# Distance-bias rows: one product for eight heads, and a store that repeats each row 128 times

## The reference

```python
bias_a = rel_bias[:, :A_HEADS]          # (32, 8)
bias_b = rel_bias[:, A_HEADS:]          # (32, 8)
...
bias = bias_table[t5_bucket(jnp.maximum(qpos[None, :, None] - sel, 0))]
s = jnp.where(valid[:, :, None, :], s + jnp.moveaxis(bias, -1, 2).astype(jnp.float32), NEG)
...
score = jnp.einsum('bqhs,bqh->bqs', jax.nn.relu(logits).astype(jnp.float32), wi)
_, sel = lax.top_k(score, topk)         # branch B: 256 keys for each query
```

## Time and profile before

| what | before |
|---|---|
| median of 3 timed runs | 3599.59 us (3599.34 to 3600.98) |
| profiled execution, its own time | 3594.39 us |
| its span, first to last instruction | 3592.7 us |
| mean granted TensorE clock | 0.968 of full |
| TensorE busy with matmuls | 3371.7 us, 94% |
| stores to `skew_scratch` | 4 of 768 KB, 3.4 us from issue to landing (median) |
| where the 16 bias products lie | 1953.5 to 1972.7 us of the span |

### The profile page before, as it was taken

How to read it: one execution, slowest core, us unless ns; L and a number is a source line. 1 busy time by engine, 2 the same in 40 slices (tenths; PEclk the granted TensorE clock), 3 DMA queues, 4 the chain that set the end, 5 groups by cost and what they waited for, 6 DMA issues and landing times.

```text
span 3592.7 us, 46841 instructions
## 1 busy us (share of the span) xinstructions
PE 3371.7 (94%) x19401; PEld 2566.3 (71%) x19401; DVE 1625.5 (45%) x3386; ACT 1121.9 (31%) x2273; POOL 457.7 (13%) x729
## 2 busy tenths in 40 slices
PE   8999999999998989999978999899999999999997
PEld 6775876777587657767646688678844588888886
DVE  3533444353344434534551699766721333323324
ACT  4432442243244333313333223366600211111112
POOL 0210120021012243203241122000000000000000
PEclk9999999999999989999987999999999999999999
DMA  2210110110011001101112123200040011111111
GB/s 97 72 36 12 42 43 1 36 28 33 18 36 42 19 15 42 42 18 42 54 39 75 37 88 94 94 1 1 1 188 12 30 48 47 59 47 48 47 47 47
DMA packets 40079, 159.61 MB, mean 44 GB/s; under 512 B 5335, under 2 KB 10009, under 8 KB 34362
## 3 DMA queue, kind: packets, MB, share of 16 engines
q1 hardware_dynamic: 39866, 156.62, 13.0%
HBM read 136.68 MB, written 19.92 MB: 44 GB/s over the span
## 4 chain that ended last, share of the span: by engine, by line
PE 78%; DVE 12%; ACT 4%; POOL 2%; issue 2%; DMA 1%; SPq 0%; POOLq 0%; ACTq 0%; DVEq 0%
PE pp L547 8%; PE pp L549 8%; PE pp L548 8%; PE pp L1180 7%; PE pp L1182 7%; PE pp L1181 7%; PE pp L717 5%; DVE xT L2224 4%; PE pp L1162 3%; PE pp L1152 3%; PE pp L868 3%; PE pp L1119 2%; PE pp L1103 2%; DVE arena L2224 2%; PE pp L647 1%
## 5 line engine op out<-in xcount | busy, mean ns | idle before, releaser
L547 PE MATMUL pp<-gx_hi,pw_hi 128*128 128x512 f32 x1616 | 664.4, 411 | 38.6 <-DVE pw_lo L1779 28.4
L549 PE MATMUL pp<-gx_hi,pw_lo 128*128 128x512 f32 x1616 | 641.2, 397 | 0.0
L548 PE MATMUL pp<-gx_lo,pw_hi 128*128 128x512 f32 x1616 | 640.4, 396 | 0.0
L547 PEld LDWEIGHTS pp<-gx_hi,pw_hi 128*128 128x128 f32 x1616 | 310.4, 192 | 113.5 <-DVE pw_lo L1779 31.6
L549 PEld LDWEIGHTS pp<-gx_hi,pw_lo 128*128 128x128 f32 x1616 | 309.4, 191 | 68.0
L548 PEld LDWEIGHTS pp<-gx_lo,pw_hi 128*128 128x128 f32 x1616 | 310.8, 192 | 60.3
L1180 PE MATMUL pp<-x_hi,wt_hi 128*128 128x512 f32 x704 | 274.1, 389 | 1.1 <-DVE x_lo L2353 1.1
L1182 PE MATMUL pp<-x_hi,wt_lo 128*128 128x512 f32 x704 | 273.9, 389 | 0.0
L1181 PE MATMUL pp<-x_lo,wt_hi 128*128 128x512 f32 x704 | 273.9, 389 | 0.0
L717 PE MATMUL pp<-xT,arena 128*128 128x512 f32 x512 | 233.8, 593 | 6.3 <-DVE arena L1955 6.3
L1779 DVE TENSOR_TENSOR pw_lo<-arena,pw_hi 128x1024 fp32r<-128x1024 f32 x73 | 89.6, 1229 | 237.9 <-ACT pw_hi L1235 237.9
(11 more groups left out here) (422 smaller groups left out, 6015.1 us busy)
## 6 DMA issues: line engine op xcount, KB each, us to landing
arena<-in_tiles_dram SPq DMA_DIRECT2D x73, 512.0 KB, 3.6
arena<-in_units_dram SPq DMA_DIRECT2D x33, 1024.0 KB, 4.9
xT<-in_tiles_dram SPq DMA_DIRECT2D x27, 512.0 KB, 4.2
xT<-in_w_outs_dram SPq DMA_DIRECT2D x6, 2048.0 KB, 8.1
arena<-gates_scratch SPq DMA_DIRECT2D x16, 512.0 KB, 4.6
gates_scratch<-arena SPq DMA_DIRECT2D x11, 512.0 KB, 5.2
arena<-in_xT_dram SPq DMA_DIRECT2D x8, 512.0 KB, 7.8
y<-in_x_dram SPq DMA_DIRECT2D x1, 4096.0 KB, 14.2
```

Source lines behind the costliest of these rows:

```text
L547: mm(b[:, hs], wh[:, c], X[0][:, k, hs], k == 0, False)
L548: mm(b[:, hs], wh[:, c], X[1][:, k, hs], False, False)
L549: m = mm(b[:, hs], wl[:, c], X[0][:, k, hs], False, k == 7)
```

## The change

The two edits belong together. A product now takes eight columns of `relb` as its stationary operand and gives eight different rows, one per partition, in 8 partitions; so there are two products (one per branch) in place of sixteen. The 128-fold repetition, which the product did before over the partitions, is now done by the store: its source is 8 partitions x 384, with a step of zero 128 times in between, and its destination the same 8 x 128 x 384 elements in DRAM as before. There are two such stores of 1536 KB in place of four of 768 KB.

```diff
-        vec = [aqT.rearrange("p t c -> p (t c)")[:, i * 1536:(i + 1) * 1536].rearrange("p (h c) -> p h c", h=4) for i in range(2)]
+        vec = [aqT[0:8, i, 0:384] for i in range(2)]
...
-            ring = Ring([4, 5])
-            for hd in range(16):
-                b = place_(ring, ("rb", hd), ("vec", hd))
-                pe.wait_ge(("d", "relb"), ("d", "oh0"), ("d", "oh1"))
-                mm(b[:, 0:384], relb[0:33, hd:hd + 1].to_broadcast([33, 128]), onehot[hd // 8], True, True).then_inc(*did("rb", hd))
+            for a in range(2):
+                b = place_(Ring([4 + a]), ("rb", a), ("vec", a))
+                pe.wait_ge(("d", "relb"), ("d", f"oh{a}"))
+                mm(b[0:8, 0:384], relb[0:33, 8 * a:8 * a + 8], onehot[a], True, True).then_inc(*did("rb", a))
...
-            for hd in range(16):
-                ac.wait_ge(("rb", hd), ("skew", hd // 4 - 2) if hd >= 8 else None)
-                act(vec[hd // 4 % 2][:, hd % 4, :], at("rb", hd)[:, 0:384], ACT.Copy).then_inc(*did("vec", hd))
+            for a in range(2):
+                evict(vec[a], at("rb", a)[0:8, 0:384], ("vec", a), ("rb", a))
...
-                    evict(aqT[:, u - 79, :], b, name, ("proj", u, 1), ("skew", 2), ("skew", 3))
+                    evict(aqT[:, u - 79, :], b, name, ("proj", u, 1), ("skew", 0), ("skew", 1))
...
-            for q in range(4):
-                sp.wait_ge(("vec", 4 * q + 3))
-                move(skew[4 * q:4 * q + 4].rearrange("h p c -> p h c"), vec[q % 2], f"skew{q % 2}", "skew", q)
+            for a in range(2):
+                sp.wait_ge(("vec", a))
+                move(skew[8 * a:8 * a + 8], vec[a].unsqueeze(1).to_broadcast([8, 128, 384]), f"skew{a}", "skew", a)
...
-                    sp.wait_ge(("skew", 2), ("skew", 3), [("ys", n) for n in range(8)])
+                    sp.wait_ge(("skew", 1), [("ys", n) for n in range(8)])
...
-            sp.wait_ge(("proj", 100, 1))
+            sp.wait_ge(("proj", 100, 1), ("skew", 0))
```

## The result

The changed kernel is slower: a median of 3607.95 us over 10 runs (3602.12 to 3612.47) against 3599.47 us over 10 runs for the kernel before, timed beside it. Two of those ten, of 4931.57 and 6839.76 us, lie far out and are not in the ratio. The ratio is 1.0024, with a 95% interval from 1.0015 to 1.0032, so +8.6 us with +5.4 to +11.5.

A forecast was written before the change was run, and what follows sets the result against it. It took TensorE, busy 94% of the span, as the bound, with tile 80's load setting the time after the change. 7.5 - 1.2 + 1.7 = +8.0 us on 3599.6 gave 3607.6, say 3608; range 3578 to 3615 us.

The forecast's parts named there:

- What TensorE saves: Bias products at L972: two in place of sixteen save 19.6 us on TensorE, with 17.9 and 21.3 as ends.
- full gain: Rival: stores read at 203 GB/s or faster, tile 80 is in time, the whole saving stands; 3580 us, chance 0.20.
- The rate of the stores: Two bias-row stores out of partitions 0 to 7: 50.8 GB/s, so 61.9 us for both.
- Tile 80 behind the stores: Tile 80's load queues behind the stores and lands at 2019.5; ACT's split of it runs 7.5 us later than before.
- One sign: On SP: both stores issued by 1956, and tile 80's load at 1959, 19.6 us earlier than before.
- Slack and restart: Index scores after tile 80's split: buffer slack used up, -1.2 us; TensorE restarting slowly after its idle time, +1.7 us.
- The rest moves with it: After the index scores: bisection begins at about 2049 in place of 2041; stretches from 2045 to 2275 keep their length.
- The other wait: Rival: tile 80 overtakes the stores, and copying out tile 79 into aqT waits for them instead; 3587 us, chance 0.05.
- A single share: Rival: the eight source partitions give 25.4 GB/s in all, tile 80 lands 69.5 us late; 3670 us, chance 0.10.

The follow-up runs named there:

- the dose between: Changed kernel with branch B's store reading every second of partitions 0 to 15, branch A's store unchanged; ratio 0.9973 against the kernel before.
- the other room: Changed kernel with the bias rows in the mask room of SBUF, so copying out tiles 79 to 82 waits for no store; ratio 1.0019 against the kernel before.
- step of 8: Changed kernel with each branch's eight rows in partitions 0, 8 to 56; 3579.39 us in one profiled execution, against a median of 3601.93 before.

## Why the prediction was right

The prediction said 3608 us with the chance of 0.45 for slower, and 3607.95 was measured. That they meet within a tenth of a us is luck, since the interval of the measurement is 6 us wide and the terms of the sum were off by up to 0.9 us each; that the path is the one that was foretold is not. Its steps:

- **What TensorE saves.** Ends of 17.9 and 21.3 us, 19.6 taken. Measured 17.8 at the split of tile 79: the lower end. The clock fell behind the two products too. Two stretches of the changed kernel, with the columns of the earlier trace rows:

```profile
1962.00:1968.00 6.00, 5.45 (x18) 3.10 (x16) 1.00 (x2) 2.35 (x5) 2.37 (x1) 0.50 0.41 48
1968.00:1970.00 2.00, 2.00 (x10) 1.24 (x7) 0.68 (x2) 0.61 (x1) 0.00 (x0) 0.88 0.43 50
```

  It stood at 0.50 until about 1968.5, some 7 us, as long as behind the sixteen products. The product price of 0.65 us held (1.38 us for two). The 1.8 us by which the term was too large did not matter, since the load and not TensorE set the time; it would have in a kernel with the full gain.
- **The rate of the stores.** 50.8 GB/s was chosen and 51.4 measured (3.146 MB over 61.2 us). That the number met is luck in part: the prediction had bounds of 25 and 203 GB/s from its rows and took two shares of eight partitions by judgement, while the share that counts is that of four neighbours. This term decided between 3580 and 3670 us. The four kernels with other source partitions, and branch B's store in the dose between, show the mechanism: the groups of partitions, not the engines, not the repetition, not the rows. The Trainium skill's 27.2 GB/s for each port (SBUF — State Buffer, Door 1, the DMA port swizzle) gave an estimate of 57.8 us and 3603.5 us; the measurement lies at 25.7 for each, and decides.
- **Tile 80 behind the stores.** Expected to land 64.6 us after the first store's issue, so that the split runs 7.5 us later than before; measured 64.5 us and 7.4. Two small errors cancel in it: data began 1.4 us after the issue, not 0.9, and streamed 61.2 us, not 61.9. That it is the queue is shown by the stores in ACT's queue. One sign did not come: both stores were to be issued by 1956 and tile 80 at 1959; on the old time line SP was busy with the pair until 1964.5, and with tile 80's issue until 1994.9. It changed nothing in the sum, because the end of the stores sets the landing.
- **Slack and restart.** -1.2 was expected for the slack and -1.4 measured (from +7.4 at the split to +6.0 at the scores). For the restart +1.7 was expected and +2.6 measured (from +6.0 to +8.6 where the bisection begins); the clock was 0.63 over the 6.6 us behind the restart, a loss of 2.4:

```profile
2028.40:2035.00 6.60, 6.60 (x18) 3.52 (x19) 4.00 (x6) 1.59 (x2) 0.93 (x2) 0.63 0.29 88
```

- **The rest moves with it.** +8.6 where the bisection begins, +7.2 at its end, +8.6 in the timed ratio. The bisection itself took 245.1 us here, 246.5 before and 248.1 with the rows in 128 partitions. Why it differs by some microseconds was not tried.
- **Rivals.** The full gain is what four kernels with other partitions show, and fails here by the rate alone. The other wait (copying out of tile 79) is excluded by the other room. A single share is excluded by the plateau.

What stays open: the kernel with 128 partitions gained 22.3 us by the ratio, and the end of its interval, 17.6, only just takes in the 17.8 that its trace shows at the split of tile 80. Its profiled span is 18.8 us shorter, but the profiled execution of before, 3594.39 us, is itself 7.5 us below the 3601.93 us that before took beside it. Of some 4 us more nothing in the traces of the changed stretch says where they come from.

## What to carry to other kernels

A store out of SBUF is priced by the partitions that it reads, not by its bytes alone: eight neighbouring rows moved at an eighth of the rate of 128, and the same eight rows laid four apart at half of it. When work is moved from a compute engine to a DMA, look at what stands behind the transfer in its queue and when it is wanted; here a weight tile that had been issued 33 us before it was wanted (1978.75, split at 2011.96) came 25 us late. And compute the repeat where it is cheap: a stationary operand with each column sixteen times cost 0.1 us on TensorE and one copy of 0.40 us on ACT, and kept the fast store, worth 30 us against the change as it was made.

## What the runs showed of the hardware

- Reads out of SBUF by a store went at 25.7 GB/s for each group of four neighbouring partitions (51.4 with two groups, 103 with four, 200 with eight). Four groups gave 102 and 103 with 8 and with 16 engines busy. Partitions 32 apart shared: eight groups 0, 8, ... 56 gave 103.
- The busy share of the engines said nothing of the rate: 0.45 at 51 GB/s in the changed kernel, 0.47 at 103, 0.53 at 200.
- Issuing a second store of this kind while the first runs held the issuing engine for long: 8.8 us on SP and 8.97 on ACT at 51 GB/s. The pair of issues took 5.35 us at 103 GB/s with the step of 8, 3.48 us at 200, and 1.38 us with sixteen source rows and 1.33 us with 128, where each engine has half as many rows of the store. On ACT it took 10 of the 17.8 us of the gain.
- The load issued next in SP's queue held SP as well: 30.27 us behind the stores at 51 GB/s, 14.93 behind those at 103 (step of 8), 5.72 at 200, 3.33 with sixteen source rows, 0.34 with 128. It landed 54.7, 28.2, 13.5, 28.2 and 5.7 us after its issue. With the stores in ACT's queue it was issued in 0.33 us and landed after 17.1.
